# Modulation rows: a 32 by 32 block transpose on VectorE and a constant stationary operand, in a fused two-block transformer kernel

## The reference

```python
silu_c, silu_cc = silu(c), silu(c_ctx)
for l in range(2):
    sh1, sc1, g1, sh2, sc2, g2 = split(silu_c @ w_mod[l] + b_mod[l], 6)
    csh1, csc1, cg1, csh2, csc2, cg2 = split(silu_cc @ w_mod[l] + b_mod[l], 6)
    m_lat, m_ctx = mixer(x_lat * (1 + sc1) + sh1, x_ctx * (1 + csc1) + csh1)
    x_lat = layer_norm(ALPHA * x_lat + (1 + g1) * m_lat)
    f_lat = swiglu(x_lat * (1 + sc2) + sh2)
    x_lat = layer_norm(ALPHA * x_lat + (1 + g2) * f_lat)
    # the same for x_ctx in layer 0
# the second block: mod = silu(c_2) @ w_mod_2[i] + b_mod_2[i], six chunks, rms norms
```

## Time and profile before

| | |
|---|---|
| median of 3 runs | 2407.88 us |
| lowest and highest | 2405.9 and 2411.49 us |
| profiled execution, first to last instruction (span) | 2408.9 us |
| time around the span | none is given: the page has the span alone |
| TensorE matmul busy | 2139.8 us, 89% |
| VectorE busy | 1199.2 us, 50% |
| ScalarE busy | 858.7 us, 36% |
| mean granted TensorE clock | 0.939 of full |

### The profile page before, as it was taken

The page is one execution under the profiler, slowest core; times in us unless marked ns, Lnnn a source line. Parts: engine busy times, 40 slices in busy tenths (PEclk is TensorE's granted clock), DMA queues, the critical chain, the costliest instruction groups (busy, mean ns, idle before and its releaser), DMA issues.

```text
span 2408.9 us, 31965 instructions
## 1 busy us (share of the span) xinstructions
PE 2139.8 (89%) x12424; PEld 1713.1 (71%) x12424; DVE 1199.2 (50%) x2038; ACT 858.7 (36%) x1366; POOL 198.9 (8%) x192
## 2 busy tenths in 40 slices
PE   4999899799989999998898979899978579966998
PEld 2777557347757777775784736789967579966997
DVE  5323344454454333334434464565666675666665
ACT  3422342253232222222433434343344643433343
POOL 0000000000110003003000000200330310031001
PEclk7999899899999999998998989999989899987999
DMA  8426104012534454645381322855532345523563
GB/s 282 141 66 212 53 12 141 28 53 88 175 105 158 168 182 141 201 147 174 117 259 53 124 66 82 271 180 180 187 122 71 122 132 167 182 89 121 165 186 105
DMA packets 280888, 331.53 MB, mean 138 GB/s; under 512 B 13319, under 2 KB 229821, under 8 KB 280765
## 3 DMA queue, kind: packets, MB, share of 16 engines
q1 hardware_dynamic: 268736, 323.05, 41.1%
q10 hardware_dynamic: 12028, 6.79, 1.1%
HBM read 328.77 MB, written 1.05 MB: 137 GB/s over the span
## 4 chain that ended last, share of the span: by engine, by line
PE 69%; DVE 10%; issue 10%; ACT 4%; DMA 3%; POOL 2%; ACTq 0%; POOLq 0%; DVEq 0%
PE ps L465 17%; PE ps L467 17%; PE ps L466 17%; PE ps L1153 3%; PE ps L342 3%; PE ps L1131 2%; DVE SL L429 2%; PE ps L1140 1%; ACT SH L423 1%; DVE SM L1224 1%; DMA RAW<-in_ffn_w 1%; PE ps L352 1%; PE ps L1300 1%; POOL S L649 1%; POOL SQ L647 1%
## 5 line engine op out<-in xcount | busy, mean ns | idle before, releaser
L429 DVE TENSOR_TENSOR SL<-RAW,SH 128x1024 fp32r<-128x1024 f32 (+3 forms) x464 | 530.7, 1147 | 898.4 <-ACT SH L423 897.2
L423 ACT ACTIVATE SH<-RAW 128x1024 fp32r<-128x1024 f32 (+3 forms) x464 | 448.9, 973 | 1074.6 <-PE ps L467 926.8
L465 PE MATMUL ps<-AH,SH 128*128 128x256 f32 (+1 forms) x2048 | 675.2, 330 | 79.1 <-DVE AL L869 29.4
L466 PE MATMUL ps<-AL,SH 128*128 128x256 f32 (+1 forms) x2048 | 666.5, 325 | 0.0
L467 PE MATMUL ps<-AH,SL 128*128 128x256 f32 (+1 forms) x2048 | 665.5, 325 | 0.0
L465 PEld LDWEIGHTS ps<-AH,SH 128*128 128x128 f32 x2048 | 399.9, 195 | 143.7 <-issue 49.4
L467 PEld LDWEIGHTS ps<-AH,SL 128*128 128x128 f32 x2048 | 399.5, 195 | 29.3
L466 PEld LDWEIGHTS ps<-AL,SH 128*128 128x128 f32 x2048 | 400.1, 195 | 27.5
L465 PE MATMUL ps<-HH,SH 128*128 128x256 f32 (+1 forms) x992 | 309.3, 312 | 7.6 <-DVE HL L739 3.8
L467 PE MATMUL ps<-HH,SL 128*128 128x256 f32 (+1 forms) x992 | 308.1, 311 | 0.0
L466 PE MATMUL ps<-HL,SH 128*128 128x256 f32 (+1 forms) x992 | 307.4, 310 | 0.0
(11 more groups left out here) (235 smaller groups left out, 2206.4 us busy)
## 6 DMA issues: line engine op xcount, KB each, us to landing
SIDE<-in_w_mod SPq DMA_DIRECT2D x45, 2048.0 KB, 8.1
RAW<-in_ffn_w SPq DMA_DIRECT2D x64, 1024.0 KB, 5.4
RAW<-in_w_in SPq DMA_DIRECT2D x44, 1024.0 KB, 5.8
RAW<-in_w_ffn_gate SPq DMA_DIRECT2D x22, 1024.0 KB, 10.2
RAW<-in_w_ffn_up SPq DMA_DIRECT2D x22, 1024.0 KB, 5.9
RAW<-in_w_ffn_down SPq DMA_DIRECT2D x16, 1024.0 KB, 5.6
RAW<-in_w_branch SPq DMA_DIRECT2D x24, 512.0 KB, 3.7
RAW<-in_w_out SPq DMA_DIRECT2D x8, 1024.0 KB, 5.4
```

The costliest lines, as they stand in the source:

```text
L423: e.activation(SH[:, m, 0:kt, :], RAW[p][:, 0:kt, o:o + P], ACT.Copy).then_inc(K.up("weight_high"), 1)
L429: e.tensor_tensor(SL[:, m, 0:kt, :], RAW[p][:, 0:kt, o:o + P], SH[:, m, 0:kt, :].bitcast(F32), ALU.subtract).then_inc(K.up("weight_low"), 1)
L465: e.matmul(ps, SH[:, m, k, :], xh, start=k == 0, stop=False)
L466: e.matmul(ps, SH[:, m, k, :], xl, start=False, stop=False)
```

## The change

The copy by ScalarE becomes a transpose of 32 by 32 blocks by VectorE, from `PS[4]` to `MODROW`. After it a block's three vectors lie along the free axis and its 32 features on partitions, so four matmuls, one for each group of 32 output partitions, gather them: the stationary operand is 32 columns of `CON` (four identity matrices of 32 stacked, which sums the four groups), the moving operand has 12 columns of `MODROW`. The selector in `CON` grows from 4 to 32 columns. The semaphore `side_row_copied` of ScalarE becomes `side_flipped` of VectorE.

```diff
-C_KEEP = 740
+C_KEEP = 768
...
-    for g in range(4):
-        for v in range(3):
-            t[32 * g + v, C_SEL + v] = 1.0
+    t[:, C_SEL:C_SEL + 32] = np.tile(np.eye(32), (4, 1))
...
+    def gather_flipped(e):
+
+        blocks = MODROW[:, :].rearrange("p (q a r) -> p q a r", q=4, a=4)
+        for a in range(4):
+            ins = e.matmul(PS[5][32 * a:32 * a + 32, 0:12], CON[:, C_SEL:C_SEL + 32], blocks[:, :, a, 0:3],
+                           start=True, stop=True)
+        return ins
...
-        def act(self, e, K, j):
+        def flip(self, e, K, j):
             e.wait_ge(sem["side_rows"], K.at("side_rows", j + 1))
-            e.activation(MODROW[:, :], PS[4][:, :], ACT.Copy).then_inc(K.up("side_row_copied"), 1)
+            e.transpose(MODROW[:, :], PS[4][:, :]).then_inc(K.up("side_flipped"), 1)
 
         def pe_turn(self, e, K, j):
-            e.wait_ge(sem["side_row_copied"], K.at("side_row_copied", j + 1))
-            for q in range(4):
-                ins = e.matmul(PS[5][:, 3 * q:3 * q + 3], MODROW[:, q * P:(q + 1) * P], CON[:, C_SEL:C_SEL + 3],
-                               start=True, stop=True)
-            ins.then_inc(K.up("side_turned"), 1)
+            e.wait_ge(sem["side_flipped"], K.at("side_flipped", j + 1))
+            gather_flipped(e).then_inc(K.up("side_turned"), 1)
...
         def act(self, e, K):
             for m in range(4):
-                if self.side and m == (0 if self.by_k or self.hold else 3):
-                    self.side.act(e, K, 0)
                 e.wait_ge(sem["products"], K.at("products", self.freed(m)))
...
         def dve(self, e, K):
             for m in range(4):
+                if self.side and m == 0 and (self.by_k or self.hold):
+                    self.side.flip(e, K, 0)
                 if self.nxt:
 
                     self.nxt.split_dve(e, K, m)
+                if self.side and m == 3 and not (self.by_k or self.hold):
+                    self.side.flip(e, K, 0)
                 e.wait_ge(sem["products"], K.at("products", m + 1))
                 self.read_dve(e, K, m)
                 if m == 3 and self.side:
```

More of the change, by code:

```diff
@@ L163 @@
            "chunk2_loaded", "chunk3_loaded", "side_loaded", "out_done"],
-    "act": ["weight_high", "act_read", "side_row_copied", "act_done", "x_normed", "modulated", "root_done",
+    "act": ["weight_high", "act_read", "act_done", "x_normed", "modulated", "root_done",
             "exp_done", "turned_copied", "branch_high", "features_copied", "queries_copied", "constants_loaded",
@@ L167 @@
             "decay_squared"],
-    "dve": ["weight_low", "dve_read", "side_added", "dve_done", "centred", "input_low", "one_minus_a2", "scanned",
+    "dve": ["weight_low", "dve_read", "side_flipped", "side_added", "dve_done", "centred", "input_low", "one_minus_a2", "scanned",
             "pooled", "max_done", "probs_ready", "branch_low", "keys_copied", "hidden_low", "var_done",
@@ L597, in act @@
         def act(self, e, K):
-            if self.side:
-                self.side.act(e, K, 0)
             for m in range(4):
@@ L1489, in act @@
         def act(self, e, K):
[L1490 to L1494, removed]
+            pass
         def dve(self, e, K):
@@ L1500, in dve @@
             for j in range(4):
+                e.wait_ge(sem["side_rows"], K.at("side_rows", j + 1))
+                e.transpose(MODROW[:, :], PS[4 + 2 * (j % 2)][:, :]).then_inc(K.up("side_flipped"), 1)
                 e.wait_ge(sem["side_turned"], K.at("side_turned", j + 1))
@@ L1515, in rows_of @@
                 if j >= 2:
-                    e.wait_ge(sem["side_row_copied"], K.at("side_row_copied", j - 1))
+                    e.wait_ge(sem["side_flipped"], K.at("side_flipped", j - 1))
                 for k in range(KT):
@@ L1526, in pe @@
                     rows_of(j + 1)
-                e.wait_ge(sem["side_row_copied"], K.at("side_row_copied", j + 1))
+                e.wait_ge(sem["side_flipped"], K.at("side_flipped", j + 1))
                 if j:
                     e.wait_ge(sem["side_added"], K.at("side_added", j))
[L1530 to L1533, removed]
+                gather_flipped(e).then_inc(K.up("side_turned"), 1)
             for b in (4, 6):
-                K.bank[b] = ("side_row_copied", K.s("side_row_copied") + 4)
+                K.bank[b] = ("side_flipped", K.s("side_flipped") + 4)
             K.bank[5] = ("side_added", K.s("side_added") + 4)
```

## The result

The changed kernel takes 2516.66 us (median of 4 runs, 2510.36 to 2520.29); the kernel before takes 2408.06. The ratio is 1.0449, 95% interval 1.0432 to 1.0466: slower, by some 108.6 us, where 126 were forecast. The profiled execution took 2520.29 us, its span is 2518.5.

The account below looks back on a forecast made before the run. TensorE, busy 89% of the span, was taken to bound the kernel. Waits less small gains made 86.7 us, the lower clock 39, together 126 on 2408.9: 2535 us, range 2490 to 2568.

Parts of the forecast that it names:

- The place decides: In 38 ordinary units TensorE would wait for ScalarE's split, VectorE's subtraction, then the transpose; some 100 us of waits.
- The steps' sizes: Last product's start to next unit's first product: 3.05 us more at 17 full units, 2.15 at 10 `Branch` units.
- the 0.26 of the earlier trace: Hand-over from VectorE's end to TensorE's first matmul, taken as 0.26 us in each delayed unit.
- The estimate of 1.24 us: Transpose length by one skill page, against 0.68 taken; would add 21 us in 38 units.
- `EarlySides` gain 0.4 us a step: Three steps of `EarlySides` were to gain 0.4 us each from the cheaper four matmuls.
- The clock: TensorE's longer idle stretches bring 1.2 GHz afterwards: 30 waits at 1.4 us, times 0.93, 39 us.
- The gather: The four new matmuls on TensorE were to take 0.4 us instead of 0.81, saving 0.4 each time.
- The held clock: Rival: TensorE stalls but its clock stays up, 2496 us; chance 0.1.
- A dear transpose or gather: Rival: stall plus a 1.23 us transpose, 2556 us, or a 0.81 us gather, 2553 us; chance 0.18.
- the wait is given back: Rival: subtractions and loads get ahead, later TensorE waits shrink, 20 us at most, 2515 us; chance 0.08.
- The faster rival: Rival: the transpose is ready when the unit's last product ends, minus 19 us, 2390 us; chance 0.03.

Follow-up runs that it names:

- the place alone, with the old copy: Kernel before with ScalarE's copy moved behind its split of the next unit's tile 3, nothing on VectorE; 2491.24 us, ratio 1.0345.
- the filled wait: Changed kernel with two or three useless float32 128x512 matmuls ahead of each ordinary unit's gather; 2464.29 us, ratio 1.0226.
- the second late flip: Changed kernel with every VectorE transpose of a unit's side done twice, at its late place; 2564.23 us, ratio 1.0634.
- the early flip: Changed kernel with VectorE's transpose moved ahead of its subtraction of the next unit's tile 3 in ordinary units; 2393.59 us, ratio 0.9931.
- five gathers: Kernel with the early flip, each unit's side gathered five times in a row instead of once; 2402.52 us, ratio 0.9973.

## Why the prediction was right, step by step

**The place decides: right, and shown.** Moving the flip takes 123 us away; the place alone, with the old copy, costs 81; a second flip costs 28 us on the path late and nothing early.

**The steps' sizes: too large, 88 us for 72** (88 is the forecast's 86.7 without the 1.2 that `EarlySides` was to gain). At full units I had 3.05 us for 2.68 (3.72 less 1.04), at `Branch` 2.15 for 1.67. Three terms were each a little off. The transpose takes 0.71 us (0.68 taken), but starts 0.08 before the subtraction's record ends. From its end to the gather it is 0.06 us, not the 0.26 of the earlier trace rows: so the 0.26 there were not this hand-over alone; what else was in them stays open. And gather and return take 0.30, not 0.4. The estimate of 1.24 us, four times the 311 ns that the Trainium skill, "VectorE: DVE Perf Modes", The three transpose paths, gives for 128x128 in bf16, is near twice what the trace has. The Trainium skill, "Vector Engine (DVE) Microarchitecture Reference", section 3.8, has the transpose at one element per cycle per lane; the trace agrees in so far as its 0.71 us are near the 0.68 of the copy of the same shape.

**`EarlySides` gain 0.4 us a step: wrong in sign.** VectorE there is in a reciprocal and four subtractions when the first rows are ready:

```profile
40.21 4.56 DVE L432 TENSOR_TENSOR SL<-RAW,SH 128x1024 fp32r<-128x1024 f32 x4
...
44.69 0.71 DVE L1501 STREAM_TRANSPOSE MODROW<-ps 128x512 f32<-128x512 f32 x1
...
45.45 0.30 PE L314 MATMUL ps<-MODROW,CON 128*32 128x12 f32 x8 [3.66 <-DVE MODROW L1501]
```

In the kernel before, the copy on ScalarE had begun at 40.48 us. By the derived scales (DER from MODT), which start at 53.32 instead of 51.39 us, the change lost 1.9 us there. I had let ScalarE's work go for free and not asked what VectorE does in that section.

**The clock: right in kind and near in size, not in its parts, so its size is partly luck.** I had 28 of 30 waits followed by the lower clock, 1.4 us each, 39 us. Of the waits of 3 us all but one were followed, by 6.8 us instead of 3.4 in some; of the ten of 2.1 us at `Branch` units only four. A us at the lower level costs 0.36 us by the filled wait, and 0.38 by the second late flip (47.6 less the steps' 28.3, for 51 us more of it). This is a mean: where the 3.4 us lie wholly in a unit's products, as after the turn at 909 us, the stretch to the next turn takes 25.4 us instead of 23.8, 1.6 more; elsewhere a part of them falls into waits. The right comparison is with the kernel before with the wider table alone, which has the same layout: its execution has 273 us at the lower level (clock 0.943, span 2399.8), the changed kernel's 396, so 123 x 0.37 = 45 us. In all but one of the runs of the kernel before the clock lies between 0.937 and 0.943; this is 2 x 0.006 x 2409 = 29 us at the lower level, some 10 us of time, and 45 is good to that.

**A term that I did not have: the layout, minus 10.** I cost the wider table at nothing. With 72 + 2 + 45 - 10 = 109 us, the 108.6 measured are met, closer than the clock's term is known. The forecast's 17 us too many are 16 of the steps and 10 of the layout, less 3 of `EarlySides` and 6 of the clock: errors both ways, which in part cancel.

**The gather.** Its 0.4 us saved a turn are 0.54 with the early flip (1.04 to 0.50). The rule that a change of tiling mode drains TensorE (the Trainium skill, "TensorEngine Tiling (Array Packing)", Key Properties) shows as some 0.1 us at each edge at most: the gather starts 0.32 us behind the last product's start instead of 0.23, and the next unit starts 0.18 later, of which a repeated gather takes 0.07. It made nothing dear here.

**The rivals.** The held clock falls with the filled wait. A dear transpose or gather falls with five gathers and the 0.71 us of the record. That the wait is given back falls too, though its 2515 us lie nearest to the 2516.66 measured: behind a wait that the lower clock doesn't follow the stretch to the next turn is as long as before (34.7 us). The faster rival named the right point, whether the flip ends ahead of the last product's end: with the early flip it does, and the kernel takes 2393.6 us, where I had 2390, 10 us of the gain through the layout. In the change as made it does not.

## What to carry to other kernels

An instruction moved to another engine takes on the waits of what stands ahead of it there: ask what that engine waits for just before, and whether that wait is released by the very work that is to follow. Here the same lines at m = 3 stood ahead of a wait on ScalarE and behind one on VectorE, and this cost 123 us; one block moved up turns the change into a gain of 0.7%, of which 0.4 come from the wider table and not from the flip. A wait of the bounding engine of 3 us cost more than half as much again in lower clock here, one of 1 us only itself; and a changed table size can move a kernel by 10 us, so give it a run of its own.

## What was not expected of the hardware

- TensorE busy without a gap with 20 float32 matmuls of three columns (40 records, 4.5 us) had the clock fall to 1.2 GHz within or behind it, as an idle stretch does. With 128x512 float32 matmuls in the wait it stayed up behind 37 of 38 turns.
- The products with `HH` and `HL` of 256 tokens take some 0.120, 0.118 or 0.114 us each by how far the region with these moving operands lies from the tiles ahead of it, 10 us over the kernel; moving all tiles together by 32 or 64 bytes changes nothing.
- 32-column matmuls of 12 columns, four groups side by side, cost 0.05 to 0.10 us per gather of four when repeated, against 0.95 us for a turn of four with 128-column stationary operands.
